# A three-part edit to a 256-token, four-layer model on one core: the order of masking and copying in mixed attention, the norms ahead of cross attention, and matmuls added behind the first experts stage

## What is computed

```python
def hybrid_layer(x, ...):                        # twice
    h = rmsnorm(x, mix_norm)
    ...                                          # h @ w_in, split into heads, rope
    o_a = nsa_attention(...)                     # 8 heads: compressed (15 keys), selected, window
    o_b = swa_sink_attention(...)                # 8 heads: a band of 128 keys, with sinks
    o_c = mla_attention(...)                     # 8 heads: latent, 64 + 32 dimensions
    g_a, g_b, g_c = jnp.split(jax.nn.sigmoid(h @ w_branch_gate), 3, axis=-1)
    x = x + (g_a * (o_a @ w_branch_a) + g_b * (o_b @ w_branch_b) + g_c * (o_c @ w_branch_c)) @ w_out
    ...                                          # feed forward, gate

def second_block(x, mem, ...):
    for layer in range(2):
        hn = rms_norm(h, norm_mix[layer])
        h = h + (even_mixer if layer % 2 == 0 else odd_mixer)(hn, ...)
        mem_n = rms_norm(mem, norm_mem[layer])
        h = h + mem_cross_attention(rms_norm(h, norm_xattn[layer]), mem_n, ...)
        h = h + peer_ffn(rms_norm(h, norm_ffn[layer]), ...)      # the experts
    return rms_norm(h, norm_final)

def rms_norm(x, w):                              # in effect
    return x * lax.rsqrt(jnp.mean(x * x, axis=-1, keepdims=True) + EPS) * w
```

## Time and profile before

| | |
|---|---|
| median of 3 runs | 2992.15 us (2991.2 to 2992.56) |
| the profiled execution, its own time | 2992.93 us |
| its span in the trace | 2991.1 us |
| mean granted TensorE clock | 0.944 |
| PE busy | 2571.5 us, 86% |
| PEld busy | 1870.8 us, 63% |
| DVE busy | 2106.0 us, 70% |
| ACT busy | 1086.5 us, 36% |
| POOL busy | 605.8 us, 20% |

### The profile page before, as it was taken

How to read it: one execution, slowest core, us unless ns; L and a number is a source line. 1 busy time by engine, 2 the same in 40 slices (tenths; PEclk the granted TensorE clock), 3 DMA queues, 4 the chain that set the end, 5 groups by cost and what they waited for, 6 DMA issues and landing times. The chain is left out here.

```text
span 2991.1 us, 35366 instructions
## 1 busy us (share of the span) xinstructions
PE 2571.5 (86%) x13032; PEld 1870.8 (63%) x13032; DVE 2106.0 (70%) x4083; ACT 1086.5 (36%) x1985; POOL 605.8 (20%) x575
## 2 busy tenths in 40 slices
PE   8999999999999999998886666669999887666776
PEld 7968998887998897797542222227788553222222
DVE  6477655647765684646888888866663799888876
ACT  4374444447444574453221111115554222111111
POOL 0000000000000000001545444440000354444442
PEclk9999999999999999999998888889999998888888
DMA  6524554451555343346999999996433999999997
GB/s 259 177 100 145 184 186 171 170 183 58 184 186 183 146 148 121 113 155 245 419 419 426 427 426 427 427 427 257 143 137 128 379 427 417 427 426 426 427 427 312
DMA packets 112492, 810.79 MB, mean 271 GB/s; under 512 B 12736, under 2 KB 12736, under 8 KB 14272
## 3 DMA queue, kind: packets, MB, share of 16 engines
q0 software_dynamic: 73728, 536.90, 42.7%
q1 hardware_dynamic: 38592, 271.63, 25.1%
HBM read 807.44 MB, written 1.05 MB: 270 GB/s over the span
## 5 line engine op out<-in xcount | busy, mean ns | idle before, releaser
L3560 PE MATMUL ps<-arena 128*128 128x512 f32 x912 | 524.5, 727 | 235.6 <-ACT arena L3456 235.6
L167 DVE TENSOR_TENSOR ring_low<-ring,parts 128x2048 fp32r<-128x2048 f32 x214 | 487.9, 2291 | 302.7 <-ACT parts L161 299.3
L488 PE MATMUL ps<-parts,parts 128*128 128x256 f32 x2528 | 569.4, 283 | 2.5 <-PEq L401 1.7
L3560 PEld LDWEIGHTS ps<-arena 128*128 128x128 f32 x912 | 203.0, 232 | 543.9 <-ACT arena L3456 316.3
L488 PE MATMUL ps<-parts,ring_low 128*128 128x256 f32 x1824 | 511.8, 281 | 0.0
L161 ACT ACTIVATE parts<-ring 128x2048 fp32r<-128x2048 f32 x214 | 406.7, 1913 | 272.2 <-PE ps L496 105.2
L496 PE MATMUL ps<-parts,parts 128*128 128x512 f32 x1344 | 440.1, 397 | 5.9 <-DVE ring_low L167 3.7
L488 PEld LDWEIGHTS ps<-parts,parts 128*128 128x128 f32 x2528 | 427.6, 189 | 3.8 <-issue 2.1
L3283 POOL DMA_INDIRECT arena<-in_experts,stage_index x276 | 321.9, 1166 | 529.6 <-PE ps L3560 236.2
L3560 PE MATMUL ps<-ring,arena 128*128 128x512 f32 x616 | 319.9, 658 | 101.2 <-ACT arena L3456 100.8
L3331 DVE CUSTOM_DVE_ANT_0 arena<-arena 128x1024 f32<-128x1024 f32 x276 | 334.1, 1227 | 96.1 <-DMA arena<-in_experts,stage_index 93.0
(11 more groups left out here) (515 smaller groups left out, 2926.4 us busy)
## 6 DMA issues: line engine op xcount, KB each, us to landing
ring<-in_stream SPq DMA_DIRECT2D x249, 1024.0 KB, 4.8
arena<-in_experts,stage_index POOLq DMA_INDIRECT x276, 22.6
ring<-in_experts,stage_index POOLq DMA_INDIRECT x236, 24.6
gain_row<-in_gain_rows SPq DMA_DIRECT2D x4, 512.0 KB, 5.8
arena<-in_mem SPq DMA_DIRECT2D x2, 1024.0 KB, 5.0
arena<-in_stream SPq DMA_DIRECT2D x2, 1024.0 KB, 8.2
par<-in_params SPq DMA_DIRECT2D x4, 386.0 KB, 4.2
x<-in_x SPq DMA_DIRECT2D x1, 1024.0 KB, 4.9
```

Source lines behind the costliest of these rows:

```text
L167: dve.tensor_tensor(k.ring_low[v % SLOTS], whole, self.high_of(v).bitcast(F32), ALU.subtract).then_inc(self.ph.sem("chunk_split"), 1)
L488: last = pe.matmul(self.ps[:, 2 * pair + f // 2, (f % 2) * T:(f % 2 + 1) * T], w[:, f * P:(f + 1) * P], x[:, k, :], start=(k == 0 and i == ...
L3560: last = pe.matmul(k.ps[:, bank + n, :], diag[:, s % ROWS, :], rows[row_of[s]][:, D + n * BLK:D + (n + 1) * BLK], start=(s % SLOTS_PER_TOK ...
```

## The change

1. In mixed attention, DVE's step b masks batch b+2 directly behind scale(b), and copies out batch b-2 behind that (and does the pieces of low-part work of steps 17 to 19 behind both).
2. The "x_" and "mem_" norms use a new class, RowNorm. It does not build the two diagonal matrices: it multiplies the two 128 x 1024 tiles of x (into a spare tile) or of the memory (in place) by y on DVE, and PE turns the scaled rows by plain transposes. The diagonal tiles are gone.
3. At the end of the experts stage of layer 0, PE's list gets ten keep_busy matmuls on bank 5 (20 records), ahead of the phase's end.

```diff
+class RowNorm(Norm):
+    def __init__(self, ph, x, gain, parts, rows, junk, tag, stat):
+        super().__init__(ph, x, gain, parts, rows[:, 0, :], junk, tag, stat)
+        self.diag, self.rows, self.sources = None, rows, [(rows, gain)]
+
+    def statistics(self, dve, link):
...
+        for m in range(MT):
+            dve.tensor_scalar(self.rows[:, m, :], self.x[:, m, :], self.y[:, m:m + 1], None, ALU.mult).then_inc(self.diag_ready, 1)
+
+    def turn(self, pe):
+        pe.wait_ge(self.diag_ready, MT)
+        super().turn(pe)
@@ mixed_attention_phase, DVE
                 for b in range(nb):
                     scale(b)
+                    if b + 2 < nb:
+                        mask(b + 2)
                     if b >= 2:
                         out(b - 2)
                     if 17 <= b <= 18:
                         branch_low(b - 17)
                     if b == 19:
                         heads_low(1, 1)
-                    if b + 2 < nb:
-                        mask(b + 2)
                     if b == 3:
                         take_hidden()
@@ cross_attention
-    norm = Norm(ph, k.x, k.p2("norm_xattn"), (x_high, k.hT_low), diag, junk=(spare[:, 0, :], spare[:, 1, :]), tag="x_", stat=8)
+    norm = RowNorm(ph, k.x, k.p2("norm_xattn"), (x_high, k.hT_low), spare, junk=(spare[:, 0, :], spare[:, 1, :]), tag="x_", stat=8)
@@ attend_phase
-        mem_norm = Norm(ph, memory, k.p2("norm_mem"), (mem_high, mem_low), mem_diag,
+        mem_norm = RowNorm(ph, memory, k.p2("norm_mem"), (mem_high, mem_low), memory,
...
                 expert.tensor(pe)
+                if layer < DEPTH - 1:
+                    k.keep_busy(pe, 5, 10)
```

More of the change, by code:

```diff
@@ L646, in statistics @@
             dve.tensor_scalar(self.diag[:, m, :], self.kern.ident[:], self.y[:, m:m + 1], None, ALU.mult).then_inc(self.diag_ready, 1)
+class RowNorm(Norm):
[3 more added lines that the diff above has]
+    def statistics(self, dve, link):
+        link(dve.tensor_tensor_reduce(self.junk[1], self.x[:, 1, :], self.x[:, 1, :], 1.0, 0.0, ALU.mult, ALU.add, self.ss[:, 1:2]))
+        dve.wait_ge(self.squares_summed, 1)
+        self.kern.rstd_vector_before(dve, self.ph, link, self.ss, self.ms, D, self.tag)
+        self.kern.rstd_vector_after(dve, self.ph, link, self.ms, self.y, self.t, self.tag)
+        for m in range(MT):
[3 more added lines that the diff above has]
+        super().turn(pe)
 class LateNorm:
@@ L2830 @@
 MIX_HIGH = 15440
-NORM_ROWS = 21600
 def cross_attention(k, ph, split, lins, expert_lin, memory, mem_norm, mem_parts, late_start, expert_loads, expert_early):
@@ L2853, in cross_attention @@
     split.home[lo.chunk0 + 3], _ = k.at_parts(SCORES_FROM + 16 * PE_KEYS, CHUNK)
-    diag, _ = k.at(NORM_ROWS, MT * P)
     bank = lambda m: 4 + 2 * m
     flat = lambda m: k.ps[:, bank(m):bank(m) + 2, :].rearrange("p a b -> p (a b)")
-    norm = Norm(ph, k.x, k.p2("norm_xattn"), (x_high, k.hT_low), diag, junk=(spare[:, 0, :], spare[:, 1, :]), tag="x_", stat=8)
+    norm = RowNorm(ph, k.x, k.p2("norm_xattn"), (x_high, k.hT_low), spare, junk=(spare[:, 0, :], spare[:, 1, :]), tag="x_", stat=8)
     def sync(sp):
@@ L3601, in attend_phase @@
         mem_low, at = k.at_parts(at, KT, T)
-        mem_diag, _ = k.at(NORM_ROWS + MT * P, MT * P)
-        mem_norm = Norm(ph, memory, k.p2("norm_mem"), (mem_high, mem_low), mem_diag,
+        mem_norm = RowNorm(ph, memory, k.p2("norm_mem"), (mem_high, mem_low), memory,
                         junk=(spare[:, 0, 0:D], spare[:, 1, 0:D]), tag="mem_", stat=32)
```

## The result

The changed kernel takes **3013.65 us** (median of 6 runs, 3008.65 to 3014.91) against 2992.2 (2991.2 to 2994.13): ratio 1.0068, 95% interval 1.0058 to 1.0079. It is slower, as forecast, but by some 20 to 21 us and not by 9.9, and so outside the range that ended at 3010.5.

What follows compares the result with a forecast made beforehand. PE bounds the kernel (busy 86%), but in mixed attention with 256 keys the loop around the engines sets the pace. Order +17.4, norms -7.0, fillers -0.5 sum to +9.9: 3002.1 us, range 2997.5 to 3010.5.

Steps and rivals of the forecast that it cites:

- The loop in mixed attention: Scores, mask, out, values, next scores close a ring; scores(8) to scores(14) take 26.63 against 23.04, +3.6 a layer.
- The early steps: Mixed attention, step 4 and the next: values held by the later out, +0.80 and +0.7, together +1.5 a layer.
- The covered steps: Mixed attention, steps 1 to 3: query and hidden extras hold PE longer than the loop, so cost nothing.
- Scores(14) to scores(19): Tail of mixed attention: values wait for the later out, +3.6 a layer, 1.6 to 4.6.
- values(14): Latent batches of the tail: values(14) start at 721.37, not 719.79, +1.6.
- The granted clock in the tail: Rival: longer PE pauses in steps 8 to 19 lower the clock, +3 a layer, 3008; chance 12%.
- The rival in which plain transposes let the clock fall: At the four norms' turns, the next PE work takes 1.5 more each, 6 in all, 3008; chance 5%.
- The norms: Four turns on PE, 1.79 less each; wait of 0.2 at memory's first norm; -7.0, bounds -7.2 and -4.5.
- The fillers: Behind the first experts stage: later fillers at full clock, turn about 0.9 earlier; net -0.5, bounds -0.9 and +0.4.
- Only the long-key batches lose: Rival: other waits already hold values in steps 4, 5, 12 to 19; 3.6 a layer stay, 2992; chance 11%.
- the earlier mask wins: Rival in mixed attention: mask and out run beside turn and ACT's copy, 2 a layer gained, 2980.6; chance 6%.

Runs made afterwards that it cites:

- order_hold: Order change of mixed attention alone plus two filler matmuls in steps 15 to 17, against the kernel before: 3012.45 us, ratio 1.0067.
- order_only: Only mask(b+2) put ahead of out(b-2) in mixed attention, against the kernel before: 3016.46 us, ratio 1.0085.
- norms_only: Only the norms changed to RowNorm in both places, old order, no new fillers, against the kernel before: 2987.34 us, ratio 0.9983.
- middle_only: The new mask order in steps 4 to 11 of mixed attention only, old order elsewhere, against the kernel before: 3006.86 us, ratio 1.0043.

## Why the prediction was wrong in size

**The loop in mixed attention: right, in each leg.** The six batches from scores(8) to scores(14) took 27.13 in attention 2 and 26.77 in attention 1 against the reckoned 26.63 (and 23.04 before): 4.88 to 5.24, 4.15, 6.07, 5.12, 3.27 and 3.28 against 4.87, 4.11, 6.03, 5.12, 3.25 and 3.25. The 5.24 has 0.36 in it that isn't the loop: in attention 2 DVE stands 0.27 ahead of out(6) with no releaser named (the "issue" at 700.88), at full clock; why is open. The early steps lost 1.58 (reckoned 1.5). The covered steps lost nothing. Scores(14) to scores(19), with the clock held, lost 3.1 (reckoned 3.6); values(14), for which the sum had 3.84 behind scores(17), came 3.88 behind. With the clock held a layer loses 8.6 and 8.9, reckoned 8.7: two layers 17.4, as forecast. That this fits so well is in part luck, since the tail was reckoned 0.5 too dear, the middle a little too cheap, and the kernel before has some 0.4 of lowered clock in each of its own drains.

**The granted clock in the tail: the step that failed.** The sum put it at nothing. I held it as a rival with 12%, at +3 a layer, 3008. Against order_hold the changed kernel loses 2.5 and 3.3 to it (94.02 and 95.22 against 91.53 and 91.90), 5.8 in all. The new pauses take PE's busy time to 0.66 of 2 us in step 15, the clock goes to 0.50, and scores(19), which DVE waits for, take twice as long, with a slower drain behind: 14.69 from scores(19) to the next phase for 12.89. My argument against it, that PE is busy again behind each pause, was a guess; what could be read was that the pauses of the kernel before had already brought 0.67 behind the loops, behind a stand of 1.79 at turn(18):

```profile
726.00:728.00 2.00, 0.42 (x8) 0.18 (x4) 1.97 (x10) 1.53 (x5) 0.00 (x0) 1.00 0.00 0
728.00:730.00 2.00, 1.78 (x15) 1.55 (x17) 1.97 (x5) 2.00 (x8) 0.00 (x0) 0.67 0.00 0
730.00:732.00 2.00, 1.82 (x13) 1.42 (x12) 2.00 (x3) 0.88 (x1) 0.00 (x0) 0.50 0.00 0
```

And my own sum put 1.6 us more of standing at values(14), shortly ahead of that place. That the rival's +3 a layer came out is luck: I had priced it as values inside the loops of six batches, where the changed kernel's clock was 1.00 in every window up to scores(17), and not at the steps of latent batches, whose scores are the longest, and in the drain.

**The rest.** The sum with that term is 17.4 + 5.8 - 7.5 = +15.7, 3007.9, against +20.3 by ratio. Between the two profiled executions the difference is 21.0, and two more dips of the clock lie outside attention, at phases whose code is unchanged: at 1180 the clock is 0.64 and 0.51 for 4 us behind a phase's start where before it was 1.00 (1.5 us lost between two marks), and in the odd mixer 0.83 where it was 1.00:

```profile
1179.46:1181.46 2.00, 1.26 (x3) 1.11 (x4) 0.76 (x5) 1.67 (x3) 0.11 (x1) 0.64 0.95 393
...
2132.97:2142.97 10.00, 7.54 (x26) 5.94 (x26) 9.47 (x6) 9.49 (x7) 0.00 (x0) 0.83 0.16 47
```

The second costs 2.2 between the turn at 2072.91 and the memory's turn at 2220.78 (147.87 against 145.64). order_only, with the same attention, has 145.64 there. With the reckoned 9.9, 5.8 and 3.7 that makes 19.4 of the 21.0; the last 1.6 are open, and the experts stages alone, apart from the shorter turns, differ by some 2.5 us between these two traces, the first longer, the second shorter. Whether the two dips recur in most runs of the changed kernel wasn't shown, since only one of them is profiled. By time, part 1 alone costs 25 (21 to 29) and not 17.4, and the other two parts bring 5 and not 7.5.

**The rule on transposes.** The rival in which plain transposes let the clock fall didn't come: the norms' turns are of 1.91 to 1.97 in their four places, and the windows over them and behind them have a clock of 1.00, in the changed kernel and in norms_only. The Trainium skill's sentence in "TensorE: Matmul & The Clock Gate", "Part 4: PE-mode transpose", that the full clock doesn't engage in transpose mode, is not what these traces show: eight transposes of 128x128 take 1.04 where the clock is 1.00 (742.03 in order_hold) and 1.88 where it is 0.50 (748.24 in the changed kernel). All these stand between ordinary matmuls; what a long row of transposes alone would do to the clock, no run here shows.

**The norms.** 1.8 less on PE at each turn; on DVE the pair is 1.42 (forecast 1.33), the wait at the memory's first norm 0.26 (forecast 0.2). In time 5, with an interval from 2.4 to 7.8 that holds the 7.0.

**The fillers.** 0.7 less to the turn in the trace, no difference in time (interval of 2.7 each way). The forecast's -0.5 stands, and couldn't be told from nothing.

**Only the long-key batches lose** falls with order_only, and **the earlier mask wins** falls with all: no phase with the new order was shorter; in steps 0 to 3 its gain is nil.

## What to carry to other kernels

When an instruction that frees a buffer is moved behind a wait, follow the ring that closes: who waits for the buffer, what stands behind that in its list, and whether that is what the moved instruction now waits for. The legs of such a ring can be read from the trace before; here they gave each distance to 0.05, but for one in attention 2. Then ask what the added standing does to TensorE's clock, and put it in the sum where, as here, the trace of before already shows a lowered clock next door; a few filler matmuls in the wait told how much of the loss was clock and how much was order.

## What was not expected of the hardware

- Behind pauses of PE the clock was at or near 0.50 for 3 to 10 us in the changed kernel and the tries with its order, and for longer in middle_only, where it stayed there although PE was busy without a pause (750 to 752). The same code in the other layer had one window of 0.50.
- The same 0.66 of 2 us of PE work was followed by a clock of 0.50 in the changed kernel (738 to 740) and of 1.00 in order_hold (744 to 746). Why, no run here shows.
- Two copies of one change differed by 2.8 us in their phases (88.46 and 91.26 in middle_only), 2.4 of them by the clock alone, more than many an edit is worth.
- Four filler records of 1.03 us in all at each of three places made a phase 2.7 to 3.3 us shorter, and six records in a place where the clock fell too, but mostly beside other engines' work, made it 0.4 shorter.
